# First block's probabilities turned by products with scaled diagonals, and new orders behind norms and at the first expert

## The reference

```python
def first_block(...):
    for l in range(2):
        proj = rms_norm(h, norm_mix[l]) @ w_in[l]
        o_hg = hgrn2_mixer(hq, hf, hi, hg, lb[l], hg_gnorm[l])
        o_nsa = nsa_mixer(...)          # gate0*o_cmp + gate1*o_slc + gate2*o_swa
        h = h + concatenate([o_hg, o_nsa]) @ w_out[l]
        gu = rms_norm(h, norm_ffn[l]) @ w_ffn_in[l]
        h = h + (silu(g_ff) * u_ff) @ w_ffn_out[l]
# in nsa_mixer, for the two branches with full scores (512 tokens):
#   p = softmax(where(causal, q @ k.T * scale, NEG));  o += sigmoid(gate) * (p @ v)
# second block, the experts: for each expert e, on the tokens x that it was given
#   y = (silu(x @ w_gate[e]) * (x @ w_up[e])) @ w_down[e]
```

## Time and profile before

| | |
|---|---|
| time, median of 3 runs | 2563.9 us (2555.7 to 2564.9) |
| the profiled execution | 2562.28 us, its span 2560.4 us |
| PE / PEld busy | 2393.3 us (93%) / 1715.1 us (67%) |
| DVE / ACT / POOL busy | 1103.8 / 680.5 / 1106.2 us |
| mean granted TensorE clock | 0.972 of full |
| chain that ended last, by engine | PE 76%, DMA 14%, DVE 6%, issue 2%, ACT 1% |

### The profile page before, as it was taken

How to read it: one execution, slowest core, us unless ns; L and a number is a source line. 1 busy time by engine, 2 the same in 40 slices (tenths; PEclk the granted TensorE clock), 3 DMA queues, 4 the chain that set the end, 5 groups by cost and what they waited for, 6 DMA issues and landing times.

```text
span 2560.4 us, 36572 instructions
## 1 busy us (share of the span) xinstructions
PE 2393.3 (93%) x12784; PEld 1715.1 (67%) x12784; DVE 1103.8 (43%) x2009; ACT 680.5 (27%) x1322; POOL 1106.2 (43%) x766
## 2 busy tenths in 40 slices
PE   7999999999999999999999999999999898888884
PEld 5878678888877787678888867777686533333331
DVE  6565765112345755764112365434465511111113
ACT  5434552111016325651110022134514200000001
POOL 4862106666775841126666765543064011111111
PEclk9999999999999998999999999999999999989997
DMA  3213003333232222013333322221135399999996
GB/s 136 81 61 99 26 11 98 94 94 98 93 97 75 74 64 70 26 36 97 98 92 96 124 84 74 83 83 58 42 99 230 141 399 406 408 405 401 408 411 259
DMA packets 78173, 373.34 MB, mean 146 GB/s; under 512 B 11232, under 2 KB 11360, under 8 KB 53344
## 3 DMA queue, kind: packets, MB, share of 16 engines
q1 hardware_dynamic: 71904, 360.14, 39.0%
q0 software_dynamic: 5280, 8.40, 1.0%
q10 hardware_dynamic: 864, 3.15, 0.3%
HBM read 367.97 MB, written 12.58 MB: 149 GB/s over the span
## 4 chain that ended last, share of the span: by engine, by line
PE 76%; DMA 14%; DVE 6%; issue 2%; ACT 1%; POOL 0%; SPq 0%; DVEq 0%; POOLq 0%; ACTq 0%
PE PS L2146 17%; PE PS L2148 17%; PE PS L2147 17%; DMA arena<-w_up 13%; PE PS L2855 4%; PE PS L2569 2%; PE PS L2598 2%; PE PS L2313 1%; PE PS L2882 1%; PE PS L2583 1%; PE PS L2191 1%; PE PS L2266 1%; PE PS L2546 1%; PE PS L2249 1%; PE PS L2661 1%
## 5 line engine op out<-in xcount | busy, mean ns | idle before, releaser
L617 POOL TENSOR_SCALAR whi<-ring 128x1024 fp32r<-128x1024 f32 x250 | 276.3, 1105 | 906.3 <-PE PS L2148 666.8
L620 POOL TENSOR_TENSOR wlo<-ring,whi 128x1024 fp32r<-128x1024 f32 x250 | 632.5, 2530 | 20.8
L2147 PE MATMUL PS<-xl,whi 128*128 128x512 f32 x1296 | 506.4, 391 | 0.0
L2146 PE MATMUL PS<-xh,whi 128*128 128x512 f32 x1232 | 491.9, 399 | 6.1 <-POOL wlo L620 5.9
L2148 PE MATMUL PS<-xh,wlo 128*128 128x512 f32 x1232 | 480.8, 390 | 0.0
L2855 PE MATMUL PS<-arena,xraw 128*64 128x512 f32 x512 | 259.0, 658 | 60.5 <-DMA arena<-w_up 54.5
L2147 PEld LDWEIGHTS PS<-xl,whi 128*128 128x128 f32 x1296 | 244.6, 189 | 50.8 <-issue 3.8
L2146 PEld LDWEIGHTS PS<-xh,whi 128*128 128x128 f32 x1232 | 231.7, 188 | 60.9 <-issue 10.9
L2148 PEld LDWEIGHTS PS<-xh,wlo 128*128 128x128 f32 x1232 | 231.6, 188 | 49.0
L2856 PE MATMUL PS<-arena,xraw 128*64 128x512 f32 x512 | 259.2, 658 | 0.0
L2855 PEld LDWEIGHTS PS<-arena,xraw 128*64 128x64 f32 x512 | 71.8, 149 | 217.6 <-issue 154.1
(11 more groups left out here) (530 smaller groups left out, 4239.2 us busy)
## 6 DMA issues: line engine op xcount, KB each, us to landing
ring<-ring_w SPq DMA_DIRECT2D x280, 512.0 KB, 3.5
arena<-w_gate SPq DMA_DIRECT2D x64, 1024.0 KB, 21.0
arena<-w_up SPq DMA_DIRECT2D x64, 1024.0 KB, 27.7
xraw<-w_down SPq DMA_DIRECT2D x32, 1024.0 KB, 29.0
arena<-w_down SPq DMA_DIRECT2D x30, 1024.0 KB, 29.2
arena<-y_dram SPq DMA_DIRECT2D x8, 512.0 KB, 7.4
xT<-xT_in SPq DMA_DIRECT2D x2, 1024.0 KB, 7.6
out<-arena SPq DMA_DIRECT2D x4, 512.0 KB, 2.6
```

The source lines that it names most:

```text
L617: nc.gpsimd.tensor_scalar(hi, ring[:, t % RING, :], 1.0, 0.0, ALU.mult, ALU.add).then_inc(sems["whi"], 1)
L620: nc.gpsimd.tensor_tensor(wlo[:, t % RING, :], ring[:, t % RING, :], hi, ALU.subtract).then_inc(sems["split"], 1)
L2146: mm(out, a[0], b[0], start=start, stop=False, skip_group_check=skip_group_check)
L2147: mm(out, a[0], b[1], start=False, stop=False, skip_group_check=skip_group_check)
```

## The change

It has four parts.

1. Behind norms: the high part of tile 3 goes to `spare[0]` and is made before the norm, at the end of the layer before; tiles 4 and 5 wait for the use of tiles 0 and 1 (`back=4`). VectorE makes chunks 0 to 4 before it scales the first result and chunks 5 and 6 before the second.
2. The dummy products before feature 7 are gone.
3. In the first block's attention ScalarE no longer scales the probabilities. VectorE makes for each full item a 128x128 diagonal, `ident` times the two factors, and TensorE multiplies the unscaled probabilities with it instead of transposing them: that product is transposed and scaled. The copies to SBUF are made by VectorE for even items and by ScalarE for odd ones. The items of the compressed branch are transposed as before.
4. At the experts `xgt_v(0, 0)` stands right behind the first eight one-hot tables, before the other eleven instructions of that part.

```diff
-    sc=72, mx=72, p=72, rc=32, ps=64, tr=72, pt=72, pv=36,
+    sc=72, mx=72, p=72, rc=0, ps=0, dg=64, tr=72, pt=36, pta=36, pv=36,
...
+        NSA_FULL = [it["k"] for it in NSA if it["kind"] == "full"]
+        diag = [memn[:, n, 0:P] for n in range(4)]
...
-            for t in range(3):
-                split(0, t, spare[2] if t == 2 else None, back=0)
+            for t in range(4):
+                split(0, t, {2: spare[2], 3: spare[0]}.get(t), back=0)
...
-                        split(base, t)
+                        split(base, t, back=4 if t < 6 else 2)
...
                 split(base, T_LAYER + 2, spare[2])
+                split(base, T_LAYER + 3, spare[0])
...
-                    it = item_at(NSA, s - 2)
-                    if it and it["kind"] == "full":
+                    it = item_at(NSA, s - NSA_T)
+                    if it and it["k"] % 2:
                         k, n = it["k"], it["n"]
-                        act_e.wait_ge(sems["rc"], nth("rc", l, it["f"] // 2 + 1))
-                        nc.scalar.activation(Pr8[k % 8][:, 0:n], Pr8[k % 8][:, 0:n], ACT.Identity,
-                                             scale=Rc[:, it["f"] % 8:it["f"] % 8 + 1]).then_inc(sems["ps"], 1)
+                        act_e.wait_ge(sems["tr"], nth("tr", l, k + 1))
+                        if k >= 4:
+                            act_e.wait_ge(sems["pv"], nth("pv", l, (k - 4) // 2 + 1))
+                        nc.scalar.activation(PT4[k % 4][:, 0:n], PS[:, 4, 0:n], ACT.Identity).then_inc(sems["pta"], 1)
...
-                    raw_tile(l, 0, kT[:, 0, :])
-                    raw_tile(l, 1, kT[:, 1, :])
                     for c in range(KO):
+                        if c in (5, 7):
+                            raw_tile(l, c // 6, kT[:, c // 6, :])
...
-                        nc.vector.tensor_tensor(Rc[:, f:f + 2], Rc[:, f:f + 2], gates[:, it["qt"], g:g + 13:12],
-                                                ALU.mult).then_inc(sems["rc"], 1)
+                        for j in range(2):
+                            n = it["f"] - 1 + j
+                            if n >= 4:
+                                v.wait_ge(sems["tr"], nth("tr", l, NSA_FULL[n - 4] + 1))
+                            nc.vector.tensor_scalar(diag[n % 4], ident, Rc[:, f + j:f + j + 1],
+                                                    gates[:, it["qt"], g + 12 * j:g + 12 * j + 1], ALU.mult, ALU.mult
+                                                    ).then_inc(sems["dg"], 1)
...
-                halves = ((spare[2], t), (whi[:, (t + 1) % 2, :], t + 1))
+                halves = ((spare[2], t), (spare[0], t + 1))
...
-                    if i == 7:
-                        keep_warm(6, 3)
...
+            def turned(l, k):
+                copied = "pta" if k % 2 else "pt"
+                pe.wait_ge(sems[copied], nth(copied, l, k // 2 + 1))
...
+                if k >= 2:
+                    turned(l, k - 2)
                 if it["kind"] == "full":
-                    pe.wait_ge(sems["ps"], nth("ps", l, it["made"][0]))
+                    pe.wait_ge(sems["dg"], nth("dg", l, it["f"] + 1))
+                    for b in range(it["nb"]):
+                        ins = mm(PS[:, 3 + k % 2, b * P:b * P + P], Pr8[k % 8][:, b * P:b * P + P], diag[it["f"] % 4],
+                                 start=True, stop=True, skip_group_check=True)
```

## The result

The changed kernel takes 2589.9 us (median of 4 runs, 2587.2 to 2591.5), the kernel before 2561.1 in the same comparison (4 runs, 2555.7 to 2564.9): 1.0113 times, 95% interval 1.0100 to 1.0126, so 28.8 us slower. The forecast was 28.3 us slower, 2592. The profiled execution has a span of 2585.3 us against 2560.4.

What follows compares the result with a forecast made beforehand. TensorE, busy for 93% of the span, was taken as the bound. Terms 51.2 - 8 (attention) - 8.6 (norms) - 1.4 (dummy products) - 4.9 (first expert) = +28.3 us gave 2592 us expected, range 2565 to 2610.

Steps and rivals of the forecast that it cites:

- the price of a product over a transpose: First block's attention: each diagonal product costs TensorE 0.16 us more than a transpose, 320 of them 51.2 us.
- The 0.25 and the 0.09: Attention: us taken from the trace for a 128x128 float32 product and for a transpose of that size on TensorE.
- What comes back: Attention: TensorE's shorter waits could return about 14 us in both layers; 8 was taken.
- worth nothing by itself, as it is not full: Attention: ScalarE losing 64 scalings a layer and gaining 36 copies changes the time by nothing.
- Nothing hides this: Attention: TensorE works in order and is full, so the products' 51.2 us are paid in the open.
- the 0 to 5 of the forecast: Attention: new waits, such as TensorE's for a diagonal, would cost 0 to 5 us if they showed.
- Cheap diagonals: Rival, attention: a product costs 0.13 us, 0.04 over a transpose, so the kernel gets faster, -16 us, 2548; chance 0.12.
- Four times a transpose: Rival, attention: a diagonal product costs 0.36 us, four times 0.09; total +63 us, 2627; chance 0.03.
- Hidden after all: Rival, attention: VectorE really leads TensorE, diagonals fill gaps, the sum is about zero, 2564 us; chance 0.05.
- The norms give all: Rival, norms: splits do not block VectorE and dummy products go whole; 26 + 5 gained, total +7, 2571 us; chance 0.12.
- my bound of -6.5 for an earlier clock: First expert: the gain could reach 6.5 us if TensorE, idle for less, gets its clock back sooner.
- Passed on whole: First expert: the 4.9 us gained at the first product reach the end, as the weight stream starts as much sooner.

Runs made afterwards that it cites:

- the control: The kernel before, unchanged, profiled a second time: 2560.9 us, ratio 0.9984 to 1.0011; its span is 2556.5 us against 2560.4 in the first profile.
- the base of the splits' experiment: Kernel before plus norms, dummy-product and first-expert parts and copies in turn, ScalarE's copy ahead of the exponential from item 8; scaling and transposes kept: 2545.3 us.
- the diagonals alone: Kernel before plus the diagonal products and the copies by VectorE and ScalarE in turn, without the other three parts: 2595.8 us, ratio 1.0110 to 1.0148.

## Why the prediction was right, and where it was not

**Part 3, forecast +43, measured +37.5.** The mechanism holds: TensorE pays for the products and gets some waits back. As 51.2 - 8 was forecast, 42.6 - 5.1 came out.
- The term that was mis-sized is the price of a product over a transpose, 0.16 us, 51.2 in all. Measured are 42.6 us more of TensorE's busy time, 0.13 each. The 0.25 and the 0.09 were each read rightly, but with different products behind them; with the same one behind both the difference is 0.13.
- "What comes back" was to be 8 us of 14, as the copies of odd items stand behind ScalarE's exponential. It is 5.1, and 12.3 with the copy at the head of the step (26.7 us of standing still before, 21.7 and 14.4). So the 14 was nearly right and the discount of 6 for the place in the queue was 7. It was a guess, and here a good one.
- The step that failed is the sentence that ScalarE's 36 copies are "worth nothing by itself, as it is not full". Of an engine that waits for others, busy time says nothing on how late an instruction comes. I named the exponential ahead of the copy and did not follow it: the rows above go from 356.37 to 359.07, 2.7 us through maximum, exponential, scaling and copy, against 1.4 that TensorE has to do meanwhile. Without the scaling it is 0.6 less, and with products 0.5 more to do for each four of them, so little is left to wait in the changed kernel (4.2 us). Where the transposes stayed, the same step would have put the forecast off by 44 us.
- "Nothing hides this" holds against the kernel before. It does not between kernels that both have the late copy: there the products cost 15 us, where they cost 34.5 with the copy early; and the late copy costs 29 without the products and 10 with them.
- The diagonals were to take some 0.23 us on VectorE; a free one takes 0.35. The prediction left open whether GpSimd's splits hold them. They do, three times a layer, to 1.4, 2.0 and 2.3 us:

```profile
308.92 2.22 DVE L1724 TENSOR_SCALAR memn<-mats,Rc,gates 128x128 f32<-128x128 f32 x2
...
308.44 2.36 POOL L622 TENSOR_TENSOR wlo<-ring,whi 128x1024 fp32r<-128x1024 f32 x1
```

The first of these two ends at 310.88 and GpSimd's instruction at 310.80. TensorE's products waited for a diagonal only twice, 1.0 us in all, within the 0 to 5 of the forecast.

Two of the signs came out weaker than forecast: TensorE is busy for 96% of the attention and not above 97, and each attention is 18.7 us longer and not 21.

**The rivals.** *Cheap diagonals* is out: that rival has a product at 0.13 and 0.04 over a transpose, and measured are 0.21 to 0.26 and 0.13 over it. *Four times a transpose* would be 0.36 a product, also out: 0.22 to 0.11 for one more in a group is twice, 1.04 to 0.54 nearly so, and the factor of the Trainium skill (TensorE: Matmul & The Clock Gate, "Terms") is not what this shape shows. *Hidden after all* is out for this change: the attentions are as much longer as TensorE's busy time is, but for 5.1 us. *The norms give all* is out too, by part 1.

**Part 1, the norms: forecast -8.6, measured some -6.** Layer 1: forecast -4.1 at tile 4. Tile 4 starts at 813.64, 14.6 us after its 799.07 of before, in a layer that begins 15.3 later: 0.7 sooner, 0.5 against the control. GpSimd did hold VectorE, but at another place than I had it, in the low parts:

```profile
796.92 1.40 DVE L1312 SCALAR_TENSOR_TENSOR xraw<-xT,lcol,rrs 128x512 f32<-128x512 f32 x2
...
799.70 10.14 DVE L1271 TENSOR_TENSOR xl<-xraw,xh 128x512 fp32r<-128x512 f32 x8
```

```profile
797.74 1.50 POOL L619 TENSOR_SCALAR whi<-ring 128x1024 fp32r<-128x1024 f32 x1 [8.52 <-DMA ring<-ring_w]
799.33 2.71 POOL L622 TENSOR_TENSOR wlo<-ring,whi 128x1024 fp32r<-128x1024 f32 x1
802.01 1.48 POOL L619 TENSOR_SCALAR whi<-ring 128x1024 fp32r<-128x1024 f32 x1
803.58 2.70 POOL L622 TENSOR_TENSOR wlo<-ring,whi 128x1024 fp32r<-128x1024 f32 x1
```

```profile
806.88 6.92 PE L2204 MATMUL PS<-xl,arena_r 128*128 128x512 f32 x14 [1.52 <-DVE xl L1271]
813.64 0.39 PE L2155 MATMUL PS<-xh,whi 128*128 128x512 f32 x1
```

Eight low parts take 10.14 us instead of 4.89; the wait of 1.98 for tile 4's split, which ended at 799.07 in before, is gone, and 1.52 plus a slow run of 14, for 3.4 us at half clock, stand in its place. The Trainium skill (SBUF — State Buffer, "SBUF: two separate sides") says that a VectorE instruction with two SBUF inputs and a GpSimd instruction that reads SBUF exclude each other for the whole instruction. These rows agree: the first and the third low part take 2.9 us each and end 0.55 after GpSimd's `wlo`, the last five, beside no split, 0.68. I had the refill of the ring at 780.9 in the old times, and it came about 1.3 us later. In another execution (the base of the splits' experiment) chunk 7 is the stretched one, at 2.27, as forecast. Layer 0 gave -3.1 against the control, forecast -1, of which 2.2 appear with the diagonals alone too, mostly by the granted clock as said above. In the profiles of the other kernels with this part the stretch to 240.31 is 1.5 to 3.3 us shorter than in before, so what it gives in layer 0 isn't shown. The second block gave -2.1, forecast -3.5, and most of those kernels repeat that (-2.0 to -2.3 in seven of the eight with both splits early).

**Part 2, forecast -1.4, measured about nothing** (-0.4 in layer 1, where the lag goes from 14.57 to 14.14, +0.2 in layer 0). As forecast, the split behind eight other instructions comes next; what the dummy products covered is now a wait:

```profile
829.67 2.37 POOL L622 TENSOR_TENSOR wlo<-ring,whi 128x1024 fp32r<-128x1024 f32 x1
...
832.17 0.49 PE L2155 MATMUL PS<-xh,whi 128*128 128x512 f32 x1 [2.02 <-POOL wlo L622]
```

**Part 4, forecast -4.9, measured -4.7 at the gate and about -3 at the end.** The wait of 5.66 is 1.34 now. But the half clock lasts longer behind it (from 2055.8 to 2062.6; in before from 2027.4 to 2037.6, most of it ahead of the gate):

```profile
2054.47 1.39 DVE L2037 TENSOR_SCALAR sq<-misc_all,slot 128x64 bf16<-128x64 f32 x8
...
2056.51 1.11 PE L2872 MATMUL PS<-arena,xraw 128*64 128x512 f32 x1 [1.34 <-DVE xraw L2033]
...
2061.69 1.06 PE L2872 MATMUL PS<-arena,xraw 128*64 128x512 f32 x1
2062.54 0.63 PE L2872 MATMUL PS<-arena,xraw 128*64 128x512 f32 x1
```

```profile
2037.68 0.59 PE L2855 MATMUL PS<-arena,xraw 128*64 128x512 f32 x1
```

Gate products start 0.85 apart until 2062.54, 6.0 us behind the first; in the kernel before (the single row) until 2037.68, 3.4 us behind. VectorE is in the one-hot tables until 2055.86, 0.7 us longer than the turn takes, which is why the wait is 1.34 and not the 0.8 of the forecast. 1.3 of the 4.7 us go there, and my bound of -6.5 for an earlier clock pointed the wrong way. "Passed on whole" did not hold.

In all the forecast 28.3 and the measured 28.8 agree because +43 for the attentions was 6 too much and the 14.9 of gains outside them 6 too much as well. The direction was right for the reason given, that TensorE pays for products and is full. That the size came out within 1 us was luck.

## What to carry to other kernels

Before work is moved to an engine that has time, write down what stands ahead of it in that engine's queue and what that waits for; put the instruction that someone waits for at the head of the step. Here the place of one 0.6 us copy was worth 10 to 49 us. When two costs lie side by side, taking one away measures neither: undo both, then one at a time. And a price that is a difference of two distances between starts needs the same kind of instruction behind both: here that is 0.13 instead of 0.16.

## What the runs showed of the hardware that I had not expected

- TensorE dropped to half clock for 10 us while busy without a gap, in one of two profiles of one program (0.51 against 1.00), and lost 3.8 us. In a single pair of profiles that reads as an effect of an edit.
- The norms of layer 1 and of the second block were 3.0 and 3.4 us longer with the diagonals alone, none of their instructions changed. In layer 1 VectorE's chunks and low parts take what they took before (7.88 and 4.89 us), and it is the clock that differs: half clock comes 2.4 us later against the work and so falls on products, and again for 3.4 us behind tile 4 (granted clock 0.50 from 816.9 to 820.3, 1.00 at the same work before), which makes 1.7 of the 3.0. The second block has such a second piece too. What sets it is open. Effects of 2 or 3 us at a norm can't be credited from one trace.
- VectorE's 128x128 diagonal, an instruction with one tensor input from SBUF, was held to the end of GpSimd's split each of the six times they met (2.3 us at most, instead of 0.35).
